# A hybrid decoder trunk on one core: high and low parts of v in one stationary tile, a PSUM bank per head, and the Fox heads' masks added by VectorE

## The chip, the cores and the metric

The kernel runs on one core of one Trainium2 chip. The metric is the device time of one execution in microseconds (us), lower is better. Three executions of the kernel before took 2653.26, 2653.28 and 2653.67 us; the median is 2653.28 us.

## What is computed

A trunk of two layers (512 tokens, 1024 channels, fp32) with three sub-layers in each: a SwiGLU feed-forward, a mixer, and a second feed-forward. The mixer projects the normed input once and feeds three branches: a gated linear recurrence, stick-breaking attention (8 heads of 64 channels) and forgetting attention ("Fox", 8 heads of 64). The change touches the two attentions, cut here to what matters:

```
# stick-breaking, per head, strictly causal (s < t)
z = q @ k.T * scale
w = exp(log_sigmoid(z) + suffix sums of log_sigmoid(-z)), 0 where s >= t
y = w @ v
# forgetting attention, per head
z = q @ k.T * scale + cum[t] - cum[s]
p = softmax(where(s <= t, z, -inf))
y = p @ v
# later: mixed += gate1 * (y_sb @ w_sb) + gate2 * (y_fox @ w_fox)
```

## The kernel before, in words

**Split numbers.** TensorE multiplies in the type fp32r, which keeps fewer bits than fp32. So every fp32 operand is held as a rounded high part and a low part (the rest), and a product is three matmuls into one PSUM bank: high by high, high by low, low by high (`mm3`, lines 1493 to 1496). Mostly ScalarE makes the high part, VectorE the low part, and each signals its own semaphore.

**Weights.** A unit is a weight tile of 128x8x128. SyncE loads it, ScalarE rounds it (`tick`, line 571), GpSimd subtracts (line 498), three units ahead of their use. A unit's 24 matmuls of 512 columns take TensorE about 5.4 us. ScalarE's program is written out by hand, so a tick stands at a fixed place among the attention's steps and runs when ScalarE gets there.

**Attention.** Each layer has 8 pairs of heads, p = 0 to 3 stick-breaking, p = 4 to 7 Fox. All engines run hand-ordered programs, each in its own order, and meet at semaphores. TensorE's order for a stick-breaking pair is:

```
scores(p); w_rg(2p); qkv(p+1, 0); qkv(p+1, 1); suffix(p, 0); suffix(p, 1)
turn_v(p); qkv(p+1, 2); w_rg(2p+1); values(p, 0); values(p, 1)
```

and for a Fox pair:

```
scores(p); gate1; qkv(p+1, 0); turn_v(p); turn(p, 0); turn(p, 1)
qkv(p+1, 1); values(p, 0); values(p, 1); qkv(p+1, 2)
```

`w_rg`, `qkv` and `gate1` are units, which fill the time in which ScalarE and VectorE work on the heads. `scores` (L1723) writes the scores of both heads to banks 4, 5, 6 (head 0) and 1, 2, 3 (head 1); for Fox pairs it then adds, per head, the decay (L1729, a picked row times ones) and the causal mask as identity times mask: three matmuls of 128, 256 and 128 columns. `suffix` (L1756, L1762) adds the stick-breaking sums, the last of them from `later_lo`, and `turn_v` (L1807) transposes v into bank 7; it waits for `k_lo` of the next pair. `turn` (L1775) transposes the Fox weights, normed by VectorE (`fx_norm`, L1343).

**Values.** `values(p, e)` is y of one head: four key blocks j with 512, 384, 256 and 128 query columns, `mm3` each, twelve matmuls. The stationary tile is 128 wide: the head's 64 columns of v, and zeros in the other 64, so both heads add into one bank (0 for stick-breaking, 7 for Fox) and each fills its own half of the partitions. Then `y_round` (ScalarE, L843) copies the bank to `ys_hi` or `yf_hi`, `y_rest` (VectorE, L1355) subtracts that from the bank, and the semaphore `ybl` says that y is done and the bank free.

**What follows y.** After `values(p-1, 1)` TensorE runs `scores(p)`, `w_rg(2p)` (bank 7) and `qkv(p+1, 0)` (bank 0, which waits for `ybl`). ScalarE goes on with a tick, then `sb_1` (absolute value L809, exp L811, ln L814 of head 0, then of head 1), a tick, `q_round`, a tick, `k_round`. VectorE goes on with `sb_softplus` (L1292 to L1306), `first_part` (L1363), `sb_sums` (L1313, L1315), the same of head 1, and in between `q_rest` (L1265) and `k_rest` (L1271, `k_lo`). For Fox pairs VectorE's `fx_max` (four row maxima per head, L1332) starts when all three banks of a head are done, ScalarE's `fx_1` (L828, exp) follows, then `fx_norm`.

Of the kernel before, what the change touches and what calls it, by code (L numbers as in the profile page):

```python
# [16 lines left out]
F32 = mybir.dt.float32  # L17
F32R = mybir.dt.float32r
# [136 lines left out]
def trunk(nc, w_units, ada_w, vecs, wf_in, wab, c_rows, x_in, out):  # L155
    with ExitStack() as ctx:
# [70 lines left out]
        ys_hi = at("ys_hi", 32768, [P, 4, T], F32R)  # L227
        ys_lo = at("ys_lo", 40960, [P, 4, T], F32R)
        part = at("part", 49152, [P, KD, T])

# [15 lines left out]
        k_lo = at("k_lo", 71680, [P, T], F32R)  # L246
        v_hi = at("v_hi", 73728, [P, TT, 2 * P], F32R)
        v_lo = at("v_lo", 77824, [P, TT, 2 * P], F32R)
        e_f = [at(f"e_f{i}", 81920 + 10240 * i, [P, NS]) for i in range(2)]
# [122 lines left out]
        vl = sig("vl", PAIRS)  # L372
        v_zero = sig("v_zero", 2)
        z_done = [sig(f"z_done{e}", 3 * PAIRS) for e in range(2)]
# [17 lines left out]
        pl = sig("pl", 3 * HEADS)  # L392
        pv_head = sig("pv_head", 2 * PAIRS)
        ybh = sig("ybh", PAIRS)
        ybl = sig("ybl", PAIRS)
# [162 lines left out]
        def _(act):  # L558
# [200 lines left out]
            def v_round(l, p):  # L759
                act.wait_ge(vt_done.sem, vt_done.at(l, p + 1))  # L760
                if p:
                    act.wait_ge(pv_head.sem, pv_head.at(l, 2 * p))
                if p == 0:
                    act.wait_ge(v_zero.sem, v_zero.at(l, 1))
                src = bank[7][:, :].rearrange("p (j e d) -> p j e d", j=TT, e=2)
                for e in range(2):
                    i = A(v_hi[:, :, e * (P + HD):e * (P + HD) + HD], src[:, :, e, :], ACT.Copy)
                i.then_inc(vh.sem, 1)
# [68 lines left out]
            def y_round(l, p):  # L837
                act.wait_ge(pv_head.sem, pv_head.at(l, 2 * p + 2))
                if p == 0:
                    act.wait_ge(yal.sem, yal.at(l, KD))  # L840
                if p == 4:
                    act.wait_ge(unit_done.sem, unit_done.at(l, U_WRG(KD - 1) + 1))
                A((ys_hi if p < 4 else yf_hi)[:, p % 4, :], bank[Y_BANK(p)][:, :], ACT.Copy).then_inc(ybh.sem, 1)  # L843

# [165 lines left out]
        def _(dve):  # L1010
# [263 lines left out]
            def v_rest(l, p):  # L1274
                if p == 0:
                    dve.wait_ge(v_zero.sem, v_zero.at(l, 2))
                dve.wait_ge(vh.sem, vh.at(l, p + 1))
                src = bank[7][:, :].rearrange("p (j e d) -> p j e d", j=TT, e=2)
                for e in range(2):
                    o = e * (P + HD)  # L1280
                    i = V.tensor_tensor(v_lo[:, :, o:o + HD], src[:, :, e, :], v_hi[:, :, o:o + HD].bitcast(F32),
                                        ALU.subtract)
                i.then_inc(vl.sem, 1)
# [42 lines left out]
            def fx_max(l, p, e):  # L1326
                n = 2 * (p - 4) + e
                dve.wait_ge(pv_head.sem, pv_head.at(l, 2 * p + e - 1))
                dve.wait_ge(z_done[e].sem, z_done[e].at(l, 3 * p + 3))
                for i in range(TT):  # L1330
                    b, o = FX_AT[i]
                    V.tensor_reduce(negmax[:, e, i:i + 1], bank[ZB[e][b]][:, o:o + P * (i + 1)], AX.X, ALU.max,  # L1332
                                    negate=True).then_inc(max_ready.sem, 1)
# [17 lines left out]

            def y_rest(l, p):
                dve.wait_ge(ybh.sem, ybh.at(l, p + 1))
                hi, lo = (ys_hi, ys_lo) if p < 4 else (yf_hi, yf_lo)
                V.tensor_tensor(lo[:, p % 4, :], bank[Y_BANK(p)][:, :], hi[:, p % 4, :].bitcast(F32),  # L1355
                                ALU.subtract).then_inc(ybl.sem, 1)
# [55 lines left out]
            for l in range(DEPTH):  # L1412
# [18 lines left out]
                V.memset(v_hi[:, :, :].bitcast(F32), 0.0).then_inc(v_zero.sem, 1)  # L1431
                V.memset(v_lo[:, :, :].bitcast(F32), 0.0).then_inc(v_zero.sem, 1)
                for p in range(4):
# [58 lines left out]
        def _(pe):  # L1492
# [199 lines left out]
            def scores(l, p):  # L1692
# [38 lines left out]
                for e in range(2):  # L1731
                    z = [bank[b] for b in ZB[e]]
                    if p >= 4:
                        h = pick[:, 2 * p + e - HEADS:2 * p + e - HEADS + 1].to_broadcast([P, P])
                        add(z[0], h, decay[:, :])
                        add(z[0][:, 3 * P:], ident_r[:, :], mask_fx[:, :]).then_inc(z_done[e].sem, 1)
                        add(z[1][:, 0:3 * P], h, decay[:, 0:3 * P])
                        add(z[1][:, 3 * P:], h, decay[:, 0:P])
                        add(z[1][:, 2 * P:], ident_r[:, :], mask_fx[:, :].unsqueeze(1).to_broadcast([P, 2, P])).then_inc(z_done[e].sem, 1)
                        add(z[2][:, 0:2 * P], h, decay[:, 0:2 * P])  # L1740
                        add(z[2][:, P:2 * P], ident_r[:, :], mask_fx[:, :]).then_inc(z_done[e].sem, 1)

# [100 lines left out]
            def w_rg(l, n):  # L1843
# [145 lines left out]

def Y_BANK(p):  # L1990
    return 0 if p < 4 else 7

# [116 lines left out]
```

## Time and profile before

| what | value |
|---|---|
| median of 3 executions | 2653.28 us |
| the profiled execution, its time | 2653.1 us |
| its span in the trace | 2651.3 us |
| TensorE busy | 2636.5 us, 99% |
| VectorE, ScalarE, GpSimd busy | 46%, 39%, 44% |
| mean granted TensorE clock | 0.999 |

The span is the time from the first to the last instruction of the trace; 1.8 us of the execution lie outside it. A matmul's busy time overlaps with the next one's, so the distance from one start to the next is what a matmul costs.

### The profile page before, as it was taken

Reading aid. Unit: us, or ns where it says so; the run is one execution under the profiler, and the core shown is the slowest. Engines: PE = TensorE matmul, PEld = TensorE weight load, DVE = VectorE, ACT = ScalarE, POOL = GpSimd, SP = SyncE. Lnnn points to the kernel's source line nnn. Section 1 sums busy time; section 2 is a strip of 40 time slices with the busy share of each in tenths; the row PEclk is TensorE's granted clock in tenths of the full one; section 3 lists DMA queues with packets and bytes.
Section 4 is the critical chain, followed back from the end, with each engine's and each line's share of the span. In section 5 each row is a group of like instructions: output and inputs, shape, how many; then the busy total and the mean of one; then the engine's idle time right before and its main releaser. Section 6 shows DMA issues by size and latency. Waiting matters only on the chain.

```text
span 2651.3 us, 31680 instructions
## 1 busy us (share of the span) xinstructions
PE 2636.5 (99%) x13012; PEld 2226.0 (84%) x13012; DVE 1232.2 (46%) x1666; ACT 1036.5 (39%) x1593; POOL 1167.6 (44%) x484
## 2 busy tenths in 40 slices
PE   9999999999999999999999999999999999999998
PEld 7888888888888898888898888988888888988887
DVE  6555337866642243411165553567755423453111
ACT  6222235675444243222242222466653432422222
POOL 5555544533223435544345554344332244454443
PEclk9999999999999999999999999999999999999999
DMA  8555532222122225423345555322221222253322
GB/s 315 197 196 191 169 133 81 99 75 72 64 64 80 90 80 190 143 96 103 96 168 190 196 201 168 102 81 96 80 68 61 64 96 95 84 199 126 101 96 80
DMA packets 90833, 323.81 MB, mean 122 GB/s; under 512 B 10048, under 2 KB 12480, under 8 KB 90432
## 3 DMA queue, kind: packets, MB, share of 16 engines
q1 hardware_dynamic: 90688, 321.78, 36.0%
q8 instruction: 103, 1.69, 0.3%
q14 instruction: 42, 0.34, 0.0%
HBM read 319.64 MB, written 2.10 MB: 121 GB/s over the span
## 4 chain that ended last, share of the span: by engine, by line
PE 98%; DMA 1%; DVE 1%; ACT 0%; SPq 0%; issue 0%; ACTq 0%; DVEq 0%
PE bank L1494 30%; PE bank L1496 30%; PE bank L1495 30%; PE bank L1529 3%; PE bank L1536 1%; PE bank L1723 1%; PE bank L1756 1%; PE bank L1775 1%; PE bank L1729 1%; DMA ada<-ada_w 1%; PE bank L1591 0%; PE bank L1807 0%; PE bank L1585 0%; PE bank L1579 0%; PE bank L1762 0%; PE bank L1571 0%
## 5 line engine op out<-in xcount | busy, mean ns | idle before, releaser
L498 POOL TENSOR_TENSOR w_lo<-raw,w_hi 128x1024 fp32r<-128x1024 f32 x434 | 1121.1, 2595 | 1340.2 <-ACT w_hi L571 1339.9
L1494 PE MATMUL bank<-h_hi,w_hi 128*128 128x512 f32 x2224 | 867.8, 390 | 0.1
L1496 PE MATMUL bank<-h_hi,w_lo 128*128 128x512 f32 x2224 | 865.6, 389 | 0.0
L1495 PE MATMUL bank<-h_lo,w_hi 128*128 128x512 f32 x2224 | 865.4, 389 | 0.0
L571 ACT ACTIVATE w_hi<-raw 128x1024 fp32r<-128x1024 f32 x434 | 458.5, 1058 | 928.5 <-PE bank L1496 830.2
L1496 PEld LDWEIGHTS bank<-h_hi,w_lo 128*128 128x128 f32 x2224 | 417.4, 188 | 86.9
L1494 PEld LDWEIGHTS bank<-h_hi,w_hi 128*128 128x128 f32 x2224 | 417.5, 188 | 86.3 <-issue 0.4
L1495 PEld LDWEIGHTS bank<-h_lo,w_hi 128*128 128x128 f32 x2224 | 417.6, 188 | 85.9
L1017 DVE CUSTOM_DVE_ANT_0 ada<-ada,c_act 128x1024 f32<-128x1024 f32 x144 | 241.9, 1688 | 256.3 <-DMA ada<-ada_w 256.3
L1494 PE MATMUL bank<-g_hi,w_hi 128*128 128x512 f32 (+1 forms) x792 | 290.1, 366 | 0.0
L1496 PE MATMUL bank<-g_hi,w_lo 128*128 128x512 f32 (+1 forms) x792 | 289.4, 365 | 0.0
L1495 PE MATMUL bank<-g_lo,w_hi 128*128 128x512 f32 (+1 forms) x792 | 289.4, 365 | 0.0
L1078 DVE SCALAR_TENSOR_TENSOR x<-bank,gatec,x 128x512 f32<-128x512 f32 (+1 forms) x56 | 37.4, 673 | 357.2 <-PE bank L1496 357.2
L1105 DVE TENSOR_TENSOR tmp<-tmp,bank 128x512 f32<-128x512 f32 x88 | 60.1, 684 | 241.0 <-ACT tmp L639 240.4
L1089 DVE TENSOR_TENSOR g_lo<-tmp,g_hi 128x512 fp32r<-128x512 f32 x88 | 170.7, 1943 | 0.0
L1494 PEld LDWEIGHTS bank<-g_hi,w_hi 128*128 128x128 f32 x792 | 149.3, 189 | 24.5
L1495 PEld LDWEIGHTS bank<-g_lo,w_hi 128*128 128x128 f32 x792 | 149.3, 189 | 24.1
L1496 PEld LDWEIGHTS bank<-g_hi,w_lo 128*128 128x128 f32 x792 | 149.3, 189 | 23.9
L1529 PE MATMUL bank<-h_hi,w_hi 128*128 128x256 f32 x320 | 86.9, 288 | 0.4
L1529 PE MATMUL bank<-h_hi,w_lo 128*128 128x256 f32 x320 | 85.1, 283 | 0.0
L1373 DVE TENSOR_TENSOR sg<-sg,bank 128x512 f32<-128x512 f32 x32 | 20.6, 684 | 137.4 <-PE bank L1496 137.4
L1536 PE MATMUL bank<-h_lo,w_hi 128*128 128x256 f32 x320 | 70.1, 283 | 0.0
(266 smaller groups left out, 3044.6 us busy)
## 6 DMA issues: line engine op xcount, KB each, us to landing
raw<-w_units SPq DMA_DIRECT2D x440, 512.0 KB, 3.4
ada<-ada_w SPq DMA_DIRECT2D x144, 512.0 KB, 4.5
ada<-ada_w SPq DMA_DIRECT2D x8, 1024.0 KB, 17.9
x<-x_in SPq DMA_DIRECT2D x4, 512.0 KB, 6.9
wab_raw<-wab SPq DMA_DIRECT2D x2, 1024.0 KB, 5.6
y<-fin SPq DMA_DIRECT2D x8, 256.0 KB, 2.3
c_act<-c_rows SPq DMA_DIRECT2D x1, 512.0 KB, 3.7
vec<-vecs SPq DMA_DIRECT2D x3, 92.5 KB, 3.1
```

The lines of the kernel that those rows point to most:

```text
L498: nc.gpsimd.tensor_tensor(w_lo[s][:, :, :], raw[u % RAW][:, :, :], w_hi[s][:, :, :].bitcast(F32), ALU.subtract).then_inc(unit_lo.sem, 1)
L571: A(w_hi[n % RING][:, :, :], raw[slot][:, :, :], ACT.Copy).then_inc(unit_hi.sem, 1)
L1017: V.tensor_tensor_reduce(ada[a % 2][:, :], ada[a % 2][:, :], c_act[:, :], 1.0, 0.0, ALU.mult, ALU.add, mod[:, col:col + 1]).then_inc(ada_d ...
L1078: V.scalar_tensor_tensor(out=x[:, n, cols], in0=bnk[:, at or cols], scalar=gatec[:, n:n + 1], in1=x[:, n, cols], op0=ALU.mult, op1=ALU.add ...
L1089: V.tensor_tensor(g_lo[:, f, :], tmp[2 + f % 2][:, :], g_hi[:, f, :].bitcast(F32), ALU.subtract).then_inc(gl_ready.sem, 1)
L1105: V.tensor_tensor(tmp[2 + f % 2][:, :], tmp[f % 2][:, :], bank[F_BANK(l, s, f) + 1][:, :], ALU.mult).then_inc(g_ready.sem, 1)
L1494: nc.tensor.matmul(o, wh, xh, start=start, stop=False, skip_group_check=True)
L1495: nc.tensor.matmul(o, wh, xl, start=False, stop=False, skip_group_check=True)
L1496: return nc.tensor.matmul(o, wl, xh, start=False, stop=stop, skip_group_check=True)
L1529: nc.tensor.matmul(bank[j][:, HALF[h]], w[(u + j) % RING][:, k, :], h_hi[:, k, HALF[h]], start=h == 0 and k == 0 and w is w_hi, stop=False ...
L1536: i = nc.tensor.matmul(bank[j][:, HALF[h]], w_hi[(u + j) % RING][:, k, :], h_lo[:, k, HALF[h]], start=False, stop=k == KD - 1, skip_group_ ...
L1723: m = nc.tensor.matmul(dst[e], left[lp][r, still], right[rp][r, moving], start=p >= 4 and o == 0 and lp == 0 and rp == 0, stop=False, skip ...
```

## The change

It has two parts. **v and y:** `v_hi` and `v_lo` become one tile `v_both`. A head's stationary tile holds the high part of v in its 64 columns and the low part in the other 64, where zeros were. `values` runs two matmuls per key block, with the high and the low part of the weights as moving operand, so the head's own half of the partitions gets v_hi times the weights and the other half gets v_lo times the weights. Each head has a bank of its own (0 and 7 for stick-breaking, 7 and 4 for Fox). ScalarE copies the low half of each head's bank to SBUF, VectorE adds the main half, ScalarE rounds the sum, VectorE subtracts. (v_lo times the low part of the weights, left out before, is in it now.) Three waits are new on TensorE: `w_rg(2p)` for `ybl` of the pair before, since it writes bank 7; `values(p, 1)` of stick-breaking pairs for `first_part` of unit w_rg(2p+1), which reads bank 7; and `scores(p)` from p = 5 on for `ybl`, since it writes bank 4. One of the two memsets of v is gone. **Masks:** the identity matmuls are gone, banks 0 and 2 get their decay before bank 1, and `fx_max` adds the mask in PSUM (three additions per head) before it takes the maxima, largest block first.

```diff
-        v_hi = at("v_hi", 73728, [P, TT, 2 * P], F32R)
-        v_lo = at("v_lo", 77824, [P, TT, 2 * P], F32R)
+        v_both = at("v_both", 73728, [P, TT, 2 * P], F32R)
...
             def y_round(l, p):
-                act.wait_ge(pv_head.sem, pv_head.at(l, 2 * p + 2))
...
-                A((ys_hi if p < 4 else yf_hi)[:, p % 4, :], bank[Y_BANK(p)][:, :], ACT.Copy).then_inc(ybh.sem, 1)
+                for e in range(2):
+                    act.wait_ge(pv_head.sem, pv_head.at(l, 2 * p + e + 1))
+                    main, low = slice(HD * e, HD * e + HD), slice(HD - HD * e, P - HD * e)
+                    A(y[main, p % 4, :], bank[Y_BANKS(p)[e]][low, :], ACT.Copy).then_inc(y_low.sem, 1)
+                act.wait_ge(y_sum.sem, y_sum.at(l, 2 * p + 2))
+                A(hi[:, p % 4, :], y[:, p % 4, :], ACT.Copy).then_inc(ybh.sem, 1)
...
             def v_rest(l, p):
...
-                    o = e * (P + HD)
-                    i = V.tensor_tensor(v_lo[:, :, o:o + HD], src[:, :, e, :], v_hi[:, :, o:o + HD].bitcast(F32),
-                                        ALU.subtract)
+                    o, low = e * (P + HD), HD * (1 + e)
+                    i = V.tensor_tensor(v_both[:, :, low:low + HD], src[:, :, e, :],
+                                        v_both[:, :, o:o + HD].bitcast(F32), ALU.subtract)
...
             def fx_max(l, p, e):
...
+                z = [bank[b] for b in ZB[e]]
+                diagonal = mask_fx[:, :].bitcast(F32)
+                two = z[1][:, 2 * P:].rearrange("p (i t) -> p i t", i=2)
+                dve.wait_ge(z_done[e].sem, z_done[e].at(l, 3 * p + 1))
+                V.tensor_tensor(z[0][:, 3 * P:], z[0][:, 3 * P:], diagonal, ALU.add).then_inc(z_masked.sem, 1)
+                dve.wait_ge(z_done[e].sem, z_done[e].at(l, 3 * p + 2))
+                V.tensor_tensor(z[2][:, P:2 * P], z[2][:, P:2 * P], diagonal, ALU.add).then_inc(z_masked.sem, 1)
                 dve.wait_ge(z_done[e].sem, z_done[e].at(l, 3 * p + 3))
-                for i in range(TT):
+                V.tensor_tensor(two, two, diagonal.unsqueeze(1).to_broadcast([P, 2, P]), ALU.add)\
+                    .then_inc(z_masked.sem, 1)
+                for i in (3, 1, 2, 0):
                     b, o = FX_AT[i]
+                    dve.wait_ge(z_masked.sem, z_masked.at(l, 3 * n + (3, 2, 3, 1)[i]))
...
             def y_rest(l, p):
+                for e in range(2):
+                    main = slice(HD * e, HD * e + HD)
+                    dve.wait_ge(y_low.sem, y_low.at(l, 2 * p + e + 1))
+                    V.tensor_tensor(y[main, p % 4, :], bank[Y_BANKS(p)[e]][main, :], y[main, p % 4, :],
+                                    ALU.add).then_inc(y_sum.sem, 1)
                 dve.wait_ge(ybh.sem, ybh.at(l, p + 1))
-                V.tensor_tensor(lo[:, p % 4, :], bank[Y_BANK(p)][:, :], hi[:, p % 4, :].bitcast(F32),
+                V.tensor_tensor(lo[:, p % 4, :], y[:, p % 4, :], hi[:, p % 4, :].bitcast(F32),
                                 ALU.subtract).then_inc(ybl.sem, 1)
...
             def scores(l, p):
+                    pe.wait_ge(ybl.sem, ybl.at(l, p))
...
-                        add(z[0], h, decay[:, :])
-                        add(z[0][:, 3 * P:], ident_r[:, :], mask_fx[:, :]).then_inc(z_done[e].sem, 1)
+                        add(z[0], h, decay[:, :]).then_inc(z_done[e].sem, 1)
+                        add(z[2][:, 0:2 * P], h, decay[:, 0:2 * P]).then_inc(z_done[e].sem, 1)
                         add(z[1][:, 0:3 * P], h, decay[:, 0:3 * P])
-                        add(z[1][:, 3 * P:], h, decay[:, 0:P])
...
+                        add(z[1][:, 3 * P:], h, decay[:, 0:P]).then_inc(z_done[e].sem, 1)
...
             def values(l, p, e):
+                    if e == 1:
+                        pe.wait_ge(part_ready.sem, part_ready.at(l, 2 * p + 2))
...
-                    i = mm3(bank[Y_BANK(p)][:, P * j:T], v_hi[:, j, e * P:e * P + P], v_lo[:, j, e * P:e * P + P],
-                            e_hi[e][:, src], e_lo[e][:, src], e == 0 and j == 0, False)
+                    for weights in (e_hi[e], e_lo[e]):
+                        i = nc.tensor.matmul(bank[Y_BANKS(p)[e]][:, P * j:T], v_both[:, j, e * P:e * P + P],
+                                             weights[:, src], start=j == 0 and weights is e_hi[e], stop=False,
+                                             skip_group_check=True)
...
             def w_rg(l, n):
                 elif n % 2 == 0:
                     pe.wait_ge(part_ready.sem, part_ready.at(l, n))
+                    pe.wait_ge(ybl.sem, ybl.at(l, n // 2))
...
-def Y_BANK(p):
-    return 0 if p < 4 else 7
+def Y_BANKS(p):
+    return (0, 7) if p < 4 else (7, 4)
```

## Rows read from the trace of the kernel before

**Rows 1.** The page, busy time of TensorE: engine, us (share), instructions.

```profile
PE   2636.5 (99%) x13012; PEld 2226.0 (84%) x13012; DVE 1232.2 (46%) x1666; ACT 1036.5 (39%) x1593; POOL 1167.6 (44%) x484
```

**Rows 2.** Timeline of TensorE, pair 0's values into pair 1's scores: start us, us.

```profile
582.99 0.39 PE L1494 MATMUL bank<-e_hi,v_hi 128*128 128x512 f32 x1
...
583.44 0.39 PE L1496 MATMUL bank<-e_hi,v_lo 128*128 128x512 f32 x1
583.67 0.33 PE L1494 MATMUL bank<-e_hi,v_hi 128*128 128x384 f32 x1
...
584.85 0.44 PE L1494 MATMUL bank<-e_hi,v_hi 128*128 128x512 f32 x1
...
586.65 0.27 PE L1496 MATMUL bank<-e_hi,v_lo 128*128 128x128 f32 x1
586.86 0.44 PE L1723 MATMUL bank<-q_hi,k_hi 64*128 64x384 f32 x2
...
588.96 0.50 PE L1494 MATMUL bank<-ya_hi,w_hi 128*128 128x512 f32 x1
```

**Rows 3.** Timeline of TensorE, first scores of pairs 2, 4 and 5.

```profile
625.30 0.44 PE L1723 MATMUL bank<-q_hi,k_hi 64*128 64x384 f32 x2
...
702.16 0.50 PE L1723 MATMUL bank<-k_hi,q_hi 64*128 64x512 f32 x2
...
734.74 0.49 PE L1723 MATMUL bank<-k_hi,q_hi 64*128 64x512 f32 x2
```

**Rows 4.** Timeline of TensorE, Fox pair 4, decay and mask of one head.

```profile
704.62 0.22 PE L1729 MATMUL bank<-mask_fx,ident_r 128*128 128x128 f32 x1
704.68 0.45 PE L1729 MATMUL bank<-decay,pick 128*128 128x384 f32 x2
704.96 0.34 PE L1729 MATMUL bank<-mask_fx,ident_r 128*128 128x256 f32 x1
705.13 0.28 PE L1729 MATMUL bank<-decay,pick 128*128 128x256 f32 x1
705.25 0.22 PE L1729 MATMUL bank<-mask_fx,ident_r 128*128 128x128 f32 x1
705.31 0.44 PE L1729 MATMUL bank<-decay,pick 128*128 128x512 f32 x1
```

**Rows 5.** Groups by form: count | busy us, mean ns | idle us before.

```profile
L1494 PE MATMUL bank<-e_hi,v_hi 128*128 128x512 f32 x32 | 13.3, 416 | 0.0
...
L1729 PEld LDWEIGHTS bank<-mask_fx,ident_r 128*128 128x128 f32 x48 | 9.0, 188 | 0.0
```

**Rows 6.** Timeline of ScalarE and of VectorE after pair 0's values.

```profile
586.96 0.60 ACT L843 ACTIVATE ys_hi<-bank 128x512 fp32r<-128x512 f32 x1 [3.97 <-PE bank L1496]
...
587.59 0.69 DVE L1355 TENSOR_TENSOR ys_lo<-bank,ys_hi 128x512 fp32r<-128x512 f32 x1 [3.72 <-ACT ys_hi L843]
```

**Rows 7.** Groups by form: a copy and two subtractions.

```profile
L1379 DVE TENSOR_TENSOR mx_lo<-part,mx_hi 128x512 fp32r<-128x512 f32 x16 | 11.1, 693 | 11.2 <-ACT mx_hi L869 11.2
...
L869 ACT ACTIVATE mx_hi<-part 128x512 fp32r<-128x512 f32 x16 | 10.1, 632 | 93.6 <-DVE part L1377 93.6
...
L1349 DVE TENSOR_TENSOR e_lo<-bank,e_hi 128x256 fp32r<-128x256 f32 x16 | 6.6, 413 | 0.0
```

**Rows 8.** Timelines of GpSimd, VectorE and TensorE in pair 1.

```profile
601.80 2.50 POOL L498 TENSOR_TENSOR w_lo<-raw,w_hi 128x1024 fp32r<-128x1024 f32 x1 [1.55 <-ACT w_hi L571]
...
601.63 0.42 DVE L1298 TENSOR_TENSOR later<-e_f 128x256 f32<-128x256 f32 x1
601.97 2.42 DVE L1300 COPY later<-e_f 128x128 f32<-128x128 f32 x1
...
609.22 0.68 DVE L1271 TENSOR_TENSOR k_lo<-bank,k_hi 128x512 fp32r<-128x512 f32 x1
...
610.05 0.63 PE L1807 MATMUL bank<-ident,vt 128*128 128x128 f32 x4
```

**Rows 9.** Timelines of VectorE and TensorE in Fox pair 4, weights normed and turned.

```profile
711.73 3.46 DVE L1343 TENSOR_SCALAR e_f<-e_f,rsums 128x128 f32<-128x128 f32 x4
...
717.71 2.35 PE L1775 MATMUL bank<-ident,e_f 128*128 128x128 f32 x20
```

More of the change, by code:

```diff
@@ L228, in trunk @@
         ys_lo = at("ys_lo", 40960, [P, 4, T], F32R)
+        ys_f = at("ys_f", 40960, [P, 4, T])
+        yf_f = at("yf_f", 8192, [P, 4, T])
         part = at("part", 49152, [P, KD, T])
@@ L372, in trunk @@
         vl = sig("vl", PAIRS)
-        v_zero = sig("v_zero", 2)
+        v_zero = sig("v_zero", 1)
         z_done = [sig(f"z_done{e}", 3 * PAIRS) for e in range(2)]
@@ L393, in trunk @@
         pv_head = sig("pv_head", 2 * PAIRS)
+        y_low = sig("y_low", 2 * PAIRS)
+        y_sum = sig("y_sum", 2 * PAIRS)
+        z_masked = sig("z_masked", 3 * HEADS)
         ybh = sig("ybh", PAIRS)
@@ L766, in v_round @@
                 for e in range(2):
-                    i = A(v_hi[:, :, e * (P + HD):e * (P + HD) + HD], src[:, :, e, :], ACT.Copy)
+                    i = A(v_both[:, :, e * (P + HD):e * (P + HD) + HD], src[:, :, e, :], ACT.Copy)
                 i.then_inc(vh.sem, 1)
@@ L837, in y_round @@
             def y_round(l, p):
-                act.wait_ge(pv_head.sem, pv_head.at(l, 2 * p + 2))
+                hi, y = (ys_hi, ys_f) if p < 4 else (yf_hi, yf_f)
                 if p == 0:
@@ L1275, in v_rest @@
                 if p == 0:
-                    dve.wait_ge(v_zero.sem, v_zero.at(l, 2))
+                    dve.wait_ge(v_zero.sem, v_zero.at(l, 1))
                 dve.wait_ge(vh.sem, vh.at(l, p + 1))
@@ L1352, in y_rest @@
             def y_rest(l, p):
+                hi, lo, y = (ys_hi, ys_lo, ys_f) if p < 4 else (yf_hi, yf_lo, yf_f)
+                for e in range(2):
[3 more added lines that the diff above has]
+                                    ALU.add).then_inc(y_sum.sem, 1)
                 dve.wait_ge(ybh.sem, ybh.at(l, p + 1))
-                hi, lo = (ys_hi, ys_lo) if p < 4 else (yf_hi, yf_lo)
-                V.tensor_tensor(lo[:, p % 4, :], bank[Y_BANK(p)][:, :], hi[:, p % 4, :].bitcast(F32),
+                V.tensor_tensor(lo[:, p % 4, :], y[:, p % 4, :], hi[:, p % 4, :].bitcast(F32),
                                 ALU.subtract).then_inc(ybl.sem, 1)
@@ L1430, in _ @@
                         forget_2(l)
-                V.memset(v_hi[:, :, :].bitcast(F32), 0.0).then_inc(v_zero.sem, 1)
-                V.memset(v_lo[:, :, :].bitcast(F32), 0.0).then_inc(v_zero.sem, 1)
+                V.memset(v_both[:, :, :].bitcast(F32), 0.0).then_inc(v_zero.sem, 1)
                 for p in range(4):
@@ L1734, in scores @@
                         h = pick[:, 2 * p + e - HEADS:2 * p + e - HEADS + 1].to_broadcast([P, P])
-                        add(z[0], h, decay[:, :])
-                        add(z[0][:, 3 * P:], ident_r[:, :], mask_fx[:, :]).then_inc(z_done[e].sem, 1)
+                        add(z[0], h, decay[:, :]).then_inc(z_done[e].sem, 1)
+                        add(z[2][:, 0:2 * P], h, decay[:, 0:2 * P]).then_inc(z_done[e].sem, 1)
                         add(z[1][:, 0:3 * P], h, decay[:, 0:3 * P])
-                        add(z[1][:, 3 * P:], h, decay[:, 0:P])
-                        add(z[1][:, 2 * P:], ident_r[:, :], mask_fx[:, :].unsqueeze(1).to_broadcast([P, 2, P])).then_inc(z_done[e].sem, 1)
-                        add(z[2][:, 0:2 * P], h, decay[:, 0:2 * P])
-                        add(z[2][:, P:2 * P], ident_r[:, :], mask_fx[:, :]).then_inc(z_done[e].sem, 1)
+                        add(z[1][:, 3 * P:], h, decay[:, 0:P]).then_inc(z_done[e].sem, 1)
             def suffix(l, p, e):
```

## The prediction

> **What bounds the kernel now.** I read the page first, then the timelines of TensorE, VectorE, ScalarE and GpSimd through the attention, then the groups by form for durations. TensorE is busy for 2636.5 of 2651.3 us [rows 1], and that is real work there: in the values of pair 0 each matmul starts when its predecessor's columns have passed, 0.45 us for the two of 512 columns from 582.99 and 0.23 us for the third [rows 2]. The row groups give the same picture: between pair 1's and pair 2's scores lie 38.44 us (586.86 to 625.30), between pair 4's and pair 5's 32.58 us [rows 2, 3], and in neither did I find TensorE idle for longer than the 0.10 us at a change from 128 to 64 rows (586.65 plus the last matmul's 0.11 us, to 586.86). So a matmul taken out is time gained, as long as no other engine's chain comes out later than TensorE's order wants it. That second half is where the risk lies, because TensorE meets chains of ScalarE and VectorE with little to spare.
>
> **Values: removed work.** Before, a pair's 24 matmuls run from 582.99 to 586.86, less the 0.10 us of the change of rows: 3.77 us. One of three goes. By time a third of 3.77 us is 1.26 us per pair, 0.63 us per head. From below, only the columns count: 1280 columns at 0.23 us per 512 are 0.57 us. I take 0.63 us, since short matmuls cost more than their columns here (a head takes 1.86 us, 582.99 to 584.85, where 3 x 1280 columns would take 1.70 us). The group of the 512-column block has 32 members [rows 5], one per head, so 32 x 0.63 = **20.2 us** (18.2 at the low end). The two matmuls of a block share their stationary tile, but so did the first two of `mm3`, and they were no cheaper than the third.
>
> **Masks: removed work.** The identity matmuls occupy 0.06, 0.17 and 0.06 us by distance of starts (704.62 to 704.68, 704.96 to 705.13, 705.25 to 705.31) [rows 4]. That is 0.29 us; the matmul behind a short one starts later than its own columns explain by some 0.05 us, so I take 0.34 us. There are 48 such weight loads [rows 5], three per head, 16 heads: **5.4 us**. Low end by columns, 512 at 0.23 us: 3.7 us.
>
> The work removed is 25.6 us (low end 21.9). Dropping one memset, placing v_lo in another tile and swapping banks cost nothing on TensorE: the memset is VectorE's, before pair 0, and v_lo's two subtractions keep their shapes.
>
> **The y chain: added work.** Before: last matmul start 586.65, ScalarE's copy 586.96 to 587.56, VectorE's subtraction 587.59 to 588.28 [rows 6], hidden behind scores, w_rg only started at 588.96 [rows 2] and did not need it. Now w_rg(2p) waits for it, and the chain has four links behind the last matmul. (Head 0's low copy and addition run during head 1's matmuls, 1.25 us long.) ScalarE copies head 1's low half from 586.96, with 64 partitions but 512 columns, so I price it like the full copy; VectorE adds from 587.59 for 0.69 us; ScalarE rounds from 588.31 for 0.63 us, VectorE subtracts from 588.97 for 0.69 us [rows 7] (both SBUF to SBUF); TensorE goes at 589.75 instead of 588.96. **Stall one: 0.79 us**. It strikes pairs 1, 2 and 3 of each layer, six times: pair 0 has no y before it, pair 4 has `gate1` where w_rg stood, 1.3 us of decay later. Queued behind the wait is all of TensorE.
>
> The other queue that pays is ScalarE's: its rounding starts at 588.31 instead of 586.96, so the tick, then abs, exp and ln of both heads come 1.35 us later, and VectorE's softplus work with them. Its end is `k_lo`, done at 609.90, and `turn_v` starts at 610.05 [rows 8]. Nearly nothing is spare. TensorE itself is 0.79 us late, so the chain may slip by 0.8 to 0.9 us for free. By the rows it slips by more, though not 1.35 us: VectorE's copy L1300 sat from 601.97 to 604.39, where GpSimd's subtraction ran from 601.80 to 604.30 [rows 8]. That GpSimd piece follows `q_round`, hence TensorE, and moves to 602.59 to 605.09; L1298 moves from 601.63 to 602.98, now falls behind GpSimd's start, and waits with L1300. Both end at about 605.65 in place of 604.39: a slip of 1.26 us, `k_lo` at 611.16 against a TensorE that wants it at 610.84, plus some 0.08 us to wake. **Stall two: 0.4 us**, in the same six pairs. Together 1.2 us, **7.2 us** in all. Ends: 0.79 x 6 = 4.7 us if the softplus chain makes it; 1.35 us plus 0.1 us for a reload after the stop, 8.7 us, if it slips in full.
>
> For Fox pairs the chain of y takes the same 2.8 us, hidden by `qkv(p+1, 2)`, 5.4 us; without that cover it would be another 0.8 us or more each. At the end of pair 7 a gate unit gives the same cover. The new wait in `values(p, 1)` is met: `first_part` needs 0.9 us from the end of w_rg, `values(p, 0)` takes 1.23 us. If not, it costs the difference.
>
> **Mask additions: added work.** VectorE gets three per head. The nearest row is a 128x256 operation out of PSUM, 0.41 us [rows 7]; 128 columns I estimate at 0.28 us, so below 1.0 us per head, and the first two run beside TensorE's decay matmuls. I expect head 1's maxima 1.0 us later. Spare: VectorE's normed weights of head 1 are done at 715.19 and the turns, 2.35 us for both heads, begin at 717.71 [rows 9], so head 1's begin at 718.89, 3.7 us later; 0.7 us of that goes with the removed masks. Cost nothing, from 0 to 5.4 us.
>
> **The sum.** 20.2 + 5.4 - 7.2 = 18.4 us. The profiled execution took 2653.1 us (span 2651.3), 0.2 us under the median, which I neglect: 2653.1 - 18.4 = **2634.7 us**. Own range of this case, from 21.9 - 8.7 and 25.6 - 4.7: 2632 to 2640.
>
> **A rule against it.** VectorE's last link read PSUM and SBUF before and now reads two SBUF tiles. Rows: of VectorE's work the SBUF copy L1300 took 2.42 us beside GpSimd [rows 8]. The Trainium skill, SBUF — State Buffer, "Who interferes with whom", says the same of any VectorE instruction with two SBUF inputs against GpSimd work that reads SBUF, and that one with a single SBUF input is spared. By it `y_rest` becomes exposed. GpSimd works only after a tick, and ScalarE's next tick stands behind `y_round`, so I expect GpSimd idle then.
>
> **Rivals.**
> - *All stalls hidden* (0.08): ScalarE or VectorE is quicker on 64 partitions. 2653.1 - 25.6 = 2627.5. Against it: the four links in the rows add up.
> - *GpSimd in the way of y* (0.07): the last subtraction waits once for a GpSimd piece of 2.50 us in each of the six pairs. 15 us more: 2649.7. Against it: the order of the tick.
> - *Masks late* (0.12): VectorE's fx_max plus a GpSimd piece (L1343 took 3.46 us for four short operations [rows 9]) eats the 3.0 us to spare and the mask gain with it: 2634.7 + 5.4 = 2640.1.
> - *Slower* (0.03): TensorE in `turn_v` or w_rg waits for VectorE behind two GpSimd pieces in a row, 5.0 us per pair, six pairs, 30 us: 2664.7. It decides from 18.4 / 6 = 3.1 us more per pair. The rows show single pieces there.
> - *The split does not do as it says* (0.02): the second matmul on a tile skips its load and short ones get 0.05 us cheaper, 32 heads: 1.6 us, 2633.1.
>
> **How the numbers follow.** The forecast has 0.68. The range 2630 to 2641 takes it in with its bounds, the late masks and part of the hidden stalls, and leaves out some 0.17. A measurement of this kernel can tell about 0.2%, 5.3 us, from no change: below 2648.0 is faster. Faster: 0.68 + 0.08 + 0.12 + 0.02 = 0.90; same: 0.07; slower: 0.03.
>
> **What would show it.** Values per pair about 2.5 us; scores to scores about 30.6 us for Fox pairs (32.58 - 1.26 - 0.68) and about 38.4 us for pairs 1 to 3, where gain and stalls nearly cancel; w_rg's first matmul 2.9 us after scores began, not 2.1; a gap before `turn_v`; VectorE's L1298, not L1300, held by GpSimd. I am wrong if the stick-breaking pairs shrink by over 1 us or grow, or if gaps stand before `turn` or in Fox scores.

## The result and the profile after

Four executions of the changed kernel took 2632.69 us in the median (2632.56 to 2634.20); four of the kernel before on the same chip took 2653.27 us (2652.98 to 2653.67). The ratio is 0.9922, 95% interval 0.9909 to 0.9934: **20.6 us less**. The profiled execution took 2632.58 us, its span is 2630.6 us. One execution of the kernel before, out of seven in a later session, took 3685.04 us at a mean granted clock of 0.668, and the ratios of that session are taken without it.

The page of the kernel after; against [rows 1] TensorE has 176 matmuls fewer (128 of the values, 48 of the masks), and is still busy for 99% of the span:

```profile
span 2630.6 us, 31452 instructions
PE 2611.4 (99%) x12836; PEld 2201.3 (84%) x12836; DVE 1260.7 (48%) x1744; ACT 1056.8 (40%) x1625; POOL 1167.3 (44%) x484
```

The timeline of TensorE, kernel after: start in us, busy us, then the instruction and in brackets what ended the idle time before it. It answers to [rows 2] and to the last row of [rows 8].

```profile
582.69 0.39 PE L1818 MATMUL bank<-e_hi,v_both 128*128 128x512 f32 x1
582.92 0.39 PE L1818 MATMUL bank<-e_lo,v_both 128*128 128x512 f32 x1
583.14 0.33 PE L1818 MATMUL bank<-e_hi,v_both 128*128 128x384 f32 x1
...
585.06 0.27 PE L1818 MATMUL bank<-e_lo,v_both 128*128 128x128 f32 x1
585.26 0.44 PE L1747 MATMUL bank<-q_hi,k_hi 64*128 64x384 f32 x2
...
588.18 0.47 PE L1517 MATMUL bank<-ya_hi,w_hi 128*128 128x512 f32 x1 [0.74 <-issue]
...
609.05 0.34 PE L1783 MATMUL bank<-later_lo,nones_r 128*128 128x384 f32 x1
609.46 0.63 PE L1832 MATMUL bank<-ident,vt 128*128 128x128 f32 x4
```

Two matmuls stand on each block of the values instead of three, so the pair's values run from 582.69 to 585.26 with the 0.10 us of the change of rows: 2.47 us of work instead of 3.77. Then comes the new wait: w_rg starts 2.92 us after the pair's scores (588.18 to 585.26) instead of 2.10, and TensorE stood for 0.74 us. That unit reads `ya`, the result of the recurrence, and not the y of attention: it waits only because it writes bank 7, which y's last readers must have left. The last two rows show the second, small gap: the 384 columns of 609.05 have passed by about 609.22, `turn_v` starts at 609.46.

The chain of y on ScalarE and on VectorE, kernel after (for [rows 6]); two timelines, one fence each:

```profile
585.37 0.59 ACT L850 ACTIVATE ys_f<-bank 64x512 f32<-64x512 f32 x1 [0.61 <-PE bank L1818]
586.73 0.63 ACT L852 ACTIVATE ys_hi<-ys_f 128x512 fp32r<-128x512 f32 x1 [0.76 <-DVE ys_f L1376]
```

```profile
586.00 0.70 DVE L1376 TENSOR_TENSOR ys_f<-bank,ys_f 64x512 f32<-64x512 f32 x1 [0.52 <-ACT ys_f L850]
587.39 0.69 DVE L1379 TENSOR_TENSOR ys_lo<-ys_f,ys_hi 128x512 fp32r<-128x512 f32 x1 [0.70 <-ACT ys_hi L852]
```

Four links, each waiting for the one before: copy 585.37, addition 586.00, rounding 586.73, subtraction 587.39 to 588.08, w_rg at 588.18. The two on 64 partitions cost as much as those on 128 (0.59 us against 0.60 for the copy out of PSUM [rows 6], 0.70 against 0.69 on VectorE).

The middle of pair 1 on GpSimd and on VectorE, kernel after (for [rows 8]); L1307, L1309 and L1280 of after are L1298, L1300 and L1271 of before:

```profile
600.99 2.39 POOL L502 TENSOR_TENSOR w_lo<-raw,w_hi 128x1024 fp32r<-128x1024 f32 x1 [0.94 <-ACT w_hi L575]
```

```profile
601.43 2.23 DVE L1307 TENSOR_TENSOR later<-e_f 128x256 f32<-128x256 f32 x1
603.59 0.21 DVE L1309 COPY later<-e_f 128x128 f32<-128x128 f32 x1
...
608.63 0.68 DVE L1280 TENSOR_TENSOR k_lo<-bank,k_hi 128x512 fp32r<-128x512 f32 x1
```

Now L1307 starts behind GpSimd's piece and is held for 2.23 us (0.42 before), and the copy follows it, 0.21 us, where it was held itself before.

VectorE in Fox pair 4, kernel after: the three mask additions of head 0, the four row maxima, and the normed weights of head 1 (for [rows 9]).

```profile
702.54 0.30 DVE L1342 TENSOR_TENSOR bank<-bank,mask_fx 128x128 f32<-128x128 f32 x1
702.75 0.29 DVE L1344 TENSOR_TENSOR bank<-bank,mask_fx 128x128 f32<-128x128 f32 x1
702.95 0.42 DVE L1346 TENSOR_TENSOR bank<-bank,mask_fx 128x256 f32<-128x256 f32 x1
703.28 1.67 DVE L1351 TENSOR_REDUCE negmax<-bank 128x1 f32<-128x512 f32 x4
...
709.70 3.47 DVE L1362 TENSOR_SCALAR e_f<-e_f,rsums 128x128 f32<-128x128 f32 x4
```

The additions cost 0.74 us (702.54 to 703.28); head 1's weights are done at 713.17, and TensorE's turns start at 714.56, head 1's at about 715.74.

**Where the 20.6 us came from**, by the starts of each pair's scores (548.12, 585.26, 623.42, 661.56, 699.70 and 730.32 us in layer 1; layer 2 repeats them):

| From scores to scores | before | after | difference | times |
|---|---|---|---|---|
| pair 0 | 38.45 | 37.14 | -1.31 | 2 |
| pairs 1, 2, 3 | 38.44 | 38.15 | -0.29 | 6 |
| Fox pairs 4 to 7 | 32.58 | 30.61 | -1.97 | 8 |

In pair 0 `w_rg(0)` has no y of a pair before it to wait for, so this pair shows the values alone: 1.31 us per pair, 21.0 us in 16 pairs. The Fox pairs show the masks on top: 1.97 - 1.31 = 0.66 us, 5.3 us in 8 pairs. Pairs 1 to 3 show the stalls: 1.31 - 0.29 = 1.02 us, 6.1 us in six pairs. (Pair 7 has no scores behind it; its 1.97 us is taken over from pairs 4 to 6.) 21.0 + 5.3 - 6.1 = 20.2 us; another 0.3 us lies before the first pair's scores (548.12 against 548.41), ahead of all changed work, where the runs of this study scatter from 547.3 to 549.5.

### The profile page after: what moved, and what is told of

It reads as the page before. It is cut to its first block, busy times and chain, and to the rows that moved or that the text cites. A ratio compares the mean times of both kernels' runs of the same rounds, so it can differ in the third digit from the quotient of the medians.

```text
span 2630.6 us, 31452 instructions
## 1 busy us (share of the span) xinstructions
PE 2611.4 (99%) x12836; PEld 2201.3 (84%) x12836; DVE 1260.7 (48%) x1744; ACT 1056.8 (40%) x1625; POOL 1167.3 (44%) x484
## 4 chain that ended last, share of the span: by engine, by line
PE 98%; DVE 1%; DMA 1%; issue 0%; ACT 0%; SPq 0%; ACTq 0%; DVEq 0%
PE bank L1517 29%; PE bank L1518 29%; PE bank L1519 29%; PE bank L1552 3%; PE bank L1818 2%; PE bank L1559 1%; PE bank L1747 1%; PE bank L1777 1%; PE bank L1796 1%; DMA ada<-ada_w 1%; PE bank L1753 0%; PE bank L1832 0%; PE bank L1614 0%; PE bank L1602 0%; PE bank L1608 0%
## 5 line engine op out<-in xcount | busy, mean ns | idle before, releaser
L1397 DVE TENSOR_TENSOR sg<-sg,bank 128x512 f32<-128x512 f32 x32 | 20.6, 685 | 133.6 <-PE bank L1519 133.6
```

## The experiments

Unless an interval is given, a time is that of one execution, with a profile beside it. The kernels ran in three sessions, each beside the kernel before: 2653.33 us (one execution) beside the first four kernels below; 2654.55 us in the median of seven beside both edits, the tick behind three pairs, the added wait and the fourfold additions; 2653.28 us beside the other three. "Per pair" is the distance from scores to scores; it repeats within 0.04 us from pair to pair and layer to layer where nothing else is said, while the first scores of a kernel come anywhere from 547.3 to 549.5 us. So small differences are read from the pairs.

### Values alone, masks alone

The first kernel is the one after, with the masks of before:

```
-  V.tensor_tensor(z[0][:, 3 * P:], z[0][:, 3 * P:], diagonal, ALU.add)
...
+  add(z[0][:, 3 * P:], ident_r[:, :], mask_fx[:, :]).then_inc(z_done[e].sem, 1)
...
```

> The changed kernel with its masks put back on TensorE as identity matmuls. Theory (work on TensorE less the waits behind y): the values lose 1.31 us in each of 16 pairs, 21.0 us, and six pairs pay 1.0 us, so 2653.1 - 14.9 = about 2638.0 us; Fox pairs 31.3 us apart. Rival (the mask additions cost or bring something else than their matmuls): the difference to the changed kernel's 2632.7 us is not 5.3 us.

Measured: 2638.88 us; Fox pairs 31.30 us, pairs 1 to 3 38.15, pair 0 37.15. The total is 6.2 us over the kernel after, where 5.3 were expected; of the 0.9 us too much 0.4 lie before the first scores (548.50 against 548.12), 0.2 are in the Fox pairs, and the rest is not traced. The second is the kernel before with only the additions on VectorE in place of those matmuls (v, y and banks as before):

> The kernel before with only the masks moved to VectorE. Theory: 16 heads x 0.33 us, 5.3 us, nothing given back: 2647.8 us; Fox pairs 31.9 us apart, stick-breaking pairs unchanged at 38.44 us. Rival (VectorE's additions come late somewhere): less than 5 us, and a gap before the turns.

Measured: 2647.87 us; Fox pairs 31.88 instead of 32.58, pairs 0 to 3 at 38.44 as before. So the masks are worth 0.69 us per pair with either layout of the values (31.30 - 30.61, 32.58 - 31.88), 5.5 us, and the two halves of the change don't touch each other: every stall comes with the values.

### The first stall: what w_rg waits for

It reads nothing of y: it overwrites bank 7, and the last instruction that reads y there is VectorE's addition of head 1. The rounding and the subtraction behind it work in SBUF, so the wait for `ybl` is two links longer than the bank needs. Here TensorE waits for the addition instead:

```
-                    pe.wait_ge(ybl.sem, ybl.at(l, n // 2))
+                    pe.wait_ge(y_sum.sem, y_sum.at(l, n))
```

> The changed kernel, but w_rg(2p) waits for VectorE's addition, the last reader of bank 7, instead of for ybl two steps later. Theory of two stalls in one place each: the 0.8 us before w_rg go, ScalarE stays as late as it was, so VectorE's k_lo comes late against a TensorE that is now on time; GpSimd's second piece goes back with TensorE by 0.8 us, so the slip is about 0.3 to 0.4 us and turn_v stalls 0.25 to 0.4 us: 0.6 to 0.8 us per pair gained, 3.6 to 4.8 us, about 2628.5 us. Rival (the slip of ScalarE's chain sets the end and the stall only moves to turn_v): under 1 us gained, gap before turn_v about 1 us.

Measured: 2628.03 us, pairs 1 to 3 at 37.49 us. w_rg starts 2.11 us after the scores, as before the change. Stall one is thus worth 38.15 - 37.49 = 0.66 us per pair. The rest, 37.49 - 37.14 = 0.35 us, stays, with the gap of 0.24 us before `turn_v` at its old size and some 0.1 us in front of the last `suffix` matmuls. What TensorE meets there is `k_lo`: in the kernel before, the one after and this one `turn_v` starts 0.15 us behind the end of `k_lo`, and `k_lo` starts 22.36, 23.37 and 22.71 us behind the scores. The 0.35 us are the difference of the first and the last. VectorE's row in this kernel says where it arises:

```profile
600.80 1.58 DVE L1307 TENSOR_TENSOR later<-e_f 128x256 f32<-128x256 f32 x1
```

With scores at 584.63, it ends 17.75 us behind them, and before the change the held copy ended 17.53 us behind them (604.39 less 586.86): 0.22 us. The copy, which before was itself the held instruction, now comes behind it, another 0.13 us: 0.35 us.

### The rounding on VectorE: a shorter chain that costs 16.5 us

ScalarE makes the two low copies only; VectorE rounds y behind its own addition, so one hand-over less. ScalarE is free 1.28 us earlier (its tick starts 0.72 us behind the scores in pair 1 instead of 2.00).

```
-                act.wait_ge(y_sum.sem, y_sum.at(l, 2 * p + 2))
-                A(hi[:, p % 4, :], y[:, p % 4, :], ACT.Copy).then_inc(ybh.sem, 1)
...
+                dve.wait_ge(y_sum.sem, y_sum.at(l, 2 * p + 2))
+                V.tensor_copy(hi[:, p % 4, :], y[:, p % 4, :]).then_inc(ybh.sem, 1)
```

> The changed kernel, but VectorE rounds y (between its addition and its subtraction), and ScalarE goes on after its two low copies. Theory: ScalarE's tick and softplus chain come 1.35 us earlier, the gap before turn_v goes (0.24 us x 6); the chain to w_rg gets shorter by 0.2 us (0.43 us of VectorE in place of 0.63 us of ScalarE): about 2.6 us gained, 2630.1 us. Rival (what sets the end is ScalarE's slip, w_rg's wait is hidden behind it): over 5 us gained.

Measured: 2649.22 us; pairs 1 to 3 at 39.85 to 41.46 us. The expected time was missed by 19 us, and the result is 16.5 us worse than the kernel after. The timelines of ScalarE, GpSimd, VectorE and TensorE of this kernel, pair 1:

```profile
585.25 1.06 ACT L575 ACTIVATE w_hi<-raw 128x1024 fp32r<-128x1024 f32 x1
...
586.39 2.35 POOL L502 TENSOR_TENSOR w_lo<-raw,w_hi 128x1024 fp32r<-128x1024 f32 x1 [2.29 <-ACT w_hi L575]
...
585.99 0.43 DVE L1377 CAST ys_hi<-ys_f 128x512 fp32r<-128x512 f32 x1
586.46 2.84 DVE L1379 TENSOR_TENSOR ys_lo<-ys_f,ys_hi 128x512 fp32r<-128x512 f32 x1
...
589.39 0.47 PE L1517 MATMUL bank<-ya_hi,w_hi 128*128 128x512 f32 x1 [2.69 <-issue]
```

This is the rival "GpSimd in the way of y", which the kernel after escapes. ScalarE, done early, runs its tick at 585.25 and so hands GpSimd a piece at 586.39; VectorE's subtraction of two SBUF tiles starts 0.07 us behind it and takes 2.84 us instead of 0.69. In the kernel after the tick stands behind the rounding, and GpSimd's piece starts at 588.38, 0.30 us after the subtraction has ended:

```profile
588.38 2.41 POOL L502 TENSOR_TENSOR w_lo<-raw,w_hi 128x1024 fp32r<-128x1024 f32 x1 [3.59 <-ACT w_hi L575]
```

And a second price follows. Windows on TensorE of this kernel: stretch, its length, busy us and matmuls, granted clock, share and GB/s of the DMA.

```profile
575.00:585.00 10.00, 10.00 (x54) 1.00 0.40 135
...
589.00:592.50 3.50, 3.11 (x8) 0.63 0.46 150
...
595.00:605.00 10.00, 10.00 (x46) 1.00 0.17 52
...
1898.10:1901.60 3.50, 3.10 (x14) 1.00 0.44 150
```

```profile
590.39 0.63 PE L1517 MATMUL bank<-ya_hi,w_hi 128*128 128x512 f32 x1
590.81 0.63 PE L1518 MATMUL bank<-ya_lo,w_hi 128*128 128x512 f32 x1
...
1898.50 0.47 PE L1517 MATMUL bank<-ya_hi,w_hi 128*128 128x512 f32 x1 [2.69 <-issue]
```

After the stop of 2.69 us TensorE ran at the lower of its two clock levels: matmuls of 512 columns start 0.42 us apart (590.39 to 590.81) where they start 0.23 us apart at the full one (582.69 to 582.92 in the kernel after), for some 3.3 us. In the kernel after the granted clock behind its stop of 0.74 us is 1.00. But the low clock doesn't follow every such stop: all six are 2.69 us long, and behind the one that ends at 1898.50 (layer 2, pair 1) the granted clock is 1.00, with 14 matmuls in the 3.50 us where the first stop is followed by 8. That pair takes 39.85 us, its stop and nothing more; the five others take 41.16 to 41.46. So a stop costs its 2.69 us, and in five cases of six 1.3 to 1.6 us more. What sets the sixth apart no run here shows.

To tell the tick's place from the rounding on VectorE as the cause, the next kernel keeps the edit and gives ScalarE one wait more, ahead of its tick:

```
+                act.wait_ge(ybh.sem, ybh.at(l, p + 1))
```

> As e4_cast_dve, but ScalarE waits for VectorE's rounding of y before its next tick, so GpSimd's piece can't start before VectorE's subtraction. In e4 the subtraction took 2.84 us, GpSimd had started 0.07 us before it, and TensorE ran at half clock after the 2.7 us stop. Theory (GpSimd's start in front of the subtraction is the whole of e4's loss): the subtraction takes 0.69 us again, w_rg starts 2.7 us after scores (2.9 in the changed kernel), no half-clock rows, ScalarE still 1.1 us late: 2630 to 2632 us. Rival (rounding on VectorE is itself slow, or the half clock has another cause): stays above 2640 us.

Measured: 2630.53 us, pairs 1 to 3 at 37.95 us, w_rg 2.71 us behind the scores; no low clock. One wait took back 18.7 us, as forecast.

### Both edits together

> VectorE rounds y as in e4, and w_rg(2p) waits for the addition only, as in e3. Theory: GpSimd still holds VectorE's subtraction up by 2.2 us, but nothing waits for it until qkv(p+1, 0), 5 us later, and ScalarE's softplus chain starts 1.35 us earlier than in e3, so the gap before turn_v goes: 0.35 us x 6 under e3_wait_sum, about 2626.0 us, pairs 1 to 3 at 37.15 us like pair 0. Rival (the held subtraction delays VectorE's softplus, which comes 0.5 us behind it): gap before turn_v stays, 2628 us or more.

Measured, four executions each: 2627.39 us (2626.48 to 2627.85), ratio to the kernel before 0.9901 (0.9883 to 0.9918); pairs 1 to 3 at 37.30 us. VectorE's timeline, pair 2 of this kernel:

```profile
623.78 2.89 DVE L1379 TENSOR_TENSOR ys_lo<-ys_f,ys_hi 128x512 fp32r<-128x512 f32 x1
```

The subtraction is held as in the kernel with the rounding on VectorE alone, but no one waits for it: w_rg waits for the sum. What lengthens an instruction costs nothing until something waits for its end. The result lies between the forecast and its rival: a gap of 0.13 us before `turn_v` is left, pairs 1 to 3 miss 37.15 us by 0.15 us, and the time is 1.4 us over the 2626.0 expected.

### The tick moved ahead of y

If GpSimd's piece is in the way, let it run earlier. w_rg's tick of the next pair goes ahead of the rounding of y, on top of both edits; first behind pairs 0, 1 and 2:

```
-                    if p:
-                        tick(l, U_WRG(2 * p))
...
+                    if p < 3:
+                        tick(l, U_WRG(2 * p + 2))
```

> As e5_both, and ScalarE's tick for unit w_rg(2p+2) stands before y_round, so it runs during the values of head 0 or before, and GpSimd's piece is over when y comes. Theory: the subtraction is no longer held (0.7 us), but since nothing waited for it, no time is gained over e5: 2626.0 us within 0.5. Rival (e5 still loses time by the held subtraction): 1 us or more under e5.

Measured: 2628.56 us (2628.17 to 2629.06), ratio 0.9904 (0.9889 to 0.9920): slower by 1.2 us than the kernel with both edits beside it, where no difference was expected. Pairs 2 and 3 do come down to 37.15 us, but pair 1 takes 38.57 and 38.34. ScalarE's timeline, then TensorE's, pair 1 of this kernel:

```profile
585.51 1.06 ACT L575 ACTIVATE w_hi<-raw 128x1024 fp32r<-128x1024 f32 x1 [3.41 <-DMA raw<-w_units]
586.59 1.21 ACT L850 ACTIVATE ys_f<-bank 64x512 f32<-64x512 f32 x2
```

```profile
588.73 0.47 PE L1517 MATMUL bank<-ya_hi,w_hi 128*128 128x512 f32 x1 [1.41 <-issue]
```

The tick behind pair 0 waited for its weights' transfer, with y's copies behind it. So it was left where it was for pair 1, and moved for pairs 2 and 3 only:

```
-                    if p:
+                    if p == 1:
...
+                    if p in (1, 2):
+                        tick(l, U_WRG(2 * p + 2))
```

> As e5_both, with the earlier tick of e8_all only after pairs 1 and 2; in e8 the one after pair 0 stood 3.4 us in a wait for its weights' transfer, ScalarE's low copies of y behind it, and w_rg 1.4 us behind those, while pairs 2 and 3 ran at 37.15 us. Theory: pair 1 at 37.30 us as in e5, pairs 2 and 3 at 37.15 us: 0.6 us under e5_both, 2626 to 2627 us, a ratio of 0.990 to the kernel before. Rival (the early tick costs elsewhere, too): not under e5.

Measured: **2626.50 us** (2625.94 to 2627.97), ratio to the kernel before 0.9901 (0.9885 to 0.9918). Pairs 2 and 3 are at 37.15 us, the distance of pair 0, which has no stall: nothing is left there of what the change had added. Pair 1 keeps 0.14 us. The kernel is 26.8 us under the kernel before, where the change alone is 20.6 us under it; from the kernel with both edits its time can't be told, only its profile.

Last, the same tick with the rounding left on ScalarE: does the early tick alone close the gap before `turn_v`?

> ScalarE rounds y as in the changed kernel, w_rg(2p) waits for the addition only as in e3, and the tick stands before y_round after pairs 1 and 2. Theory (what makes turn_v late is ScalarE's slip of 1.35 us, of which the tick takes 1.05 us away): pair 1 at 37.49 us as in e3, pairs 2 and 3 at 37.15 us, no gap before turn_v there: 1.4 us under e3, 2626.5 to 2627.5 us. Rival (the gap before turn_v is GpSimd's doing whatever ScalarE does): 37.49 us in all three.

Measured: 2629.16 us (2628.22 to 2630.03), ratio 0.9910 (0.9895 to 0.9924); pair 1 at 37.49 us, pairs 2 and 3 at 37.40 us, and the gap of 0.24 us stands in all of them. The rival held in the main: of the 0.34 us the tick was to bring, it brought 0.09. (That the total lies 1.1 us over that of the kernel with the new wait alone is not the tick's doing: the first scores come 2.0 us later here, 549.51 to 547.48.) GpSimd and VectorE of this kernel, pair 2, and VectorE and GpSimd of the kernel above at the same place:

```profile
639.13 2.39 POOL L502 TENSOR_TENSOR w_lo<-raw,w_hi 128x1024 fp32r<-128x1024 f32 x1 [1.15 <-ACT w_hi L575]
...
639.36 2.44 DVE L1309 TENSOR_TENSOR later<-e_f 128x256 f32<-128x256 f32 x1
```

```profile
636.60 0.42 DVE L1307 TENSOR_TENSOR later<-e_f 128x256 f32<-128x256 f32 x1
...
636.89 2.39 POOL L502 TENSOR_TENSOR w_lo<-raw,w_hi 128x1024 fp32r<-128x1024 f32 x1 [1.68 <-ACT w_hi L575]
```

The gap of 0.24 us is there when VectorE's 256-column instruction comes behind GpSimd's start (by 0.44 us in the kernel after, 1.18 with the new wait, 0.60 with the added wait, 0.23 here), and not there when it comes ahead by 0.17 us (before the change [rows 8]) or 0.29 us (pairs 2 and 3 of the best kernel). In between stand the kernel with both edits, ahead by only 0.05 us, with a gap of 0.13, and pair 1 of the best, ahead by 0.09, with 0.09; there GpSimd's piece took 2.62 and 2.59 us instead of 2.39. The kernel with the rounding on VectorE alone doesn't count: TensorE was 4 us late there, and `k_lo` was ready 3.1 us before it. Moving this one instruction by itself wasn't tried, so its part in the gap rests on this comparison.

### How much room the masks have

Twice and four times the additions of every head. The mask is added that many times over. One thing more differs from the kernel after: the first addition waits until all three banks of the head are done, and each row maximum waits for all additions. The diff of the twofold kernel (the other has 4, 12 and 12 for 2, 6 and 6):

```
+                for r in range(2):
+                    if r:
+                        dve.wait_ge(z_masked.sem, z_masked.at(l, 6 * n + 3 * r))
...
+                    dve.wait_ge(z_masked.sem, z_masked.at(l, 6 * n + 6))
```

> The changed kernel with the mask additions made twice. In e6 three extra rounds made head 1's weights 5.7 us later, 1.9 us per round, and g1_copy as much, on which turn_v waits with 3.1 us to spare. Theory (2.5 us to spare at the turns, 3.1 us at turn_v): one extra round costs nothing, 2632.7 us within 1, Fox pairs at 30.6 us. Rival (each round costs, 36 us / 3 rounds): 2640 us or more.

Measured: 2633.07 us, Fox pairs 30.59 to 30.70 us: a second round costs nothing. It makes head 1's weights 2.3 us later: 12.27 us behind pair 4's scores (711.19 less 698.92) instead of 10.00.

> The changed kernel with the three mask additions of a Fox head made four times in a row (the masked scores become more negative, the weights stay the same), some 0.75 us more per round and head, 4.5 us later for head 1. Theory (2.5 us to spare in the changed kernel between VectorE's normed weights and head 1's turn, so one round costs nothing): it exceeds the spare time by about 2 us in each of 8 Fox pairs, with a gap between or before the turns: 14 to 20 us more, 2647 to 2653 us. Rival (the spare time is larger, the masks are far from mattering): within 2 us of 2632.7. Rival 2 (none to spare): over 30 us more.

Measured: 2668.69 us, 36 us over the kernel after; Fox pairs 33.91 to 35.04 us, the others unchanged at 38.15. The time forecast, 2647 to 2653 us, was missed by 16 us. By the number alone the second rival (no room at all) would have it, but a second round costs nothing, and that rules it out. VectorE reached head 1's weights 5.7 us later (715.42 against 709.70): 2.3 us for the first extra round with its later start, 1.7 for each of the others. But the turns were not the first to run dry. ScalarE, then TensorE of this kernel, pair 4:

```profile
716.00 0.70 ACT L858 ACTIVATE sg<-bank,vec 128x512 f32<-128x512 f32 x1
```

```profile
716.84 0.63 PE L1835 MATMUL bank<-ident,vt 128*128 128x128 f32 x4 [2.55 <-ACT sg L858]
717.30 3.98 PE L1799 MATMUL bank<-ident,e_f 128*128 128x128 f32 x20
```

and the windows of its TensorE around it:

```profile
703.00:713.00 10.00, 10.00 (x47) 1.00 0.00 0
...
716.00:721.00 5.00, 4.16 (x25) 0.68 0.29 90
...
786.00:791.00 5.00, 3.77 (x28) 1.00 0.27 88
```

`turn_v` waits for a copy of ScalarE that stands behind both heads' weights in ScalarE's queue. In the kernel after that copy is done at 710.98, 3.1 us ahead of `turn_v`; here it came 2.55 us late, and behind that stop the clock was low again: the turns took 3.98 us instead of 2.35. Three rounds more are 5.7 us, less 3.1 us of room is 2.6 us, and the stop is 2.55 us. That is so in six of the eight Fox pairs; in pair 7 of each layer another copy of ScalarE (L868) holds `turn_v`, for 3.97 us. Behind pair 6's stop, the last row shown, the clock stayed at 1.00 in both layers, and these pairs take 33.91 us where pairs 4 and 5 take 34.78 to 35.04. The 36 us are 4.5 us per Fox pair in the mean: the stop, and behind six stops of eight the low clock.

## Why the prediction was right, and where it was off

It gave 2634.7 us (2630 to 2641), 18.4 us of gain; it was 2632.7 us and 20.6 us. The mechanism held: which work goes, which two waits come, and that nothing else does. The sizes that were off, the second stall above all, were off to the same side.

- **Values**, forecast 0.63 us per head, 20.2 us: 0.655 us and 21.0 us. Short matmuls gave back slightly more than a third of the time.
- **Masks**, forecast 0.34 us per head, 5.4 us: 0.345 us and 5.5 us, by the two kernels with one part each.
- **Stall one**, forecast 0.79 us, w_rg at 2.9 us behind the scores: 2.92 us. The step was right: the lateness stays in full down to the last `suffix` matmul, which starts 23.79 us behind the scores instead of 23.01, 0.78 us later. Its removal brings only 0.66 us, because the second stall then grows from 0.23 to 0.35 us. What the prediction didn't see is that it was needless: w_rg reads no y, and the bank is free two links earlier.
- **Stall two**, forecast 0.4 us: 0.24 us, and this is the mis-sized term. The step was "Both end at about 605.65 in place of 604.39: a slip of 1.26 us". L1307 was held, as said, but the slip is 1.01 us: `k_lo` starts 23.37 us behind the scores instead of 22.36. GpSimd's piece took 2.39 us and not 2.50, and VectorE's last held work ended 0.42 us behind it (603.80 to 603.38), not 0.56. One size worked the other way: from the end of `k_lo` to `turn_v` it takes 0.15 us, not 0.08. Both stalls together: 6.1 us, not 7.2.
- **Mask additions**, cost 0: right, and the twofold kernel shows that weights another 2.3 us later cost nothing either. Their price was right too, 0.74 us for a head with the 128-column ones at 0.29 us, but not the room. The step "3.7 us later" looked at the turns; head 1's turn has 2.5 us left with the additions in (713.17 to 715.74), and in the fourfold kernel `turn_v`, with 3.1 us, was the first to stop.
- **The rule against it** was rightly weighed: GpSimd was idle then, because the tick stands behind the rounding in ScalarE's queue. The rounding on VectorE takes that cover away, and the rival came true. That it cost 16.5 us, where the rival had 15, is luck in part: the rival counted one wait of 2.50 us per pair, and what was measured is a stop 1.95 us longer plus, in five of six pairs, the low clock. The prediction gives the Trainium skill's section (SBUF — State Buffer, "Who interferes with whom") too widely: an instruction with one SBUF input is spared there only outside the modes that use both ports. The SBUF copy L1300, with one input, was held for 2.42 us [rows 8]. *All stalls hidden* would have been 2627.5 us; the kernels that remove both stalls, but for 0.14 us in some pairs, reach 2626.5 and 2627.4.

## What to carry to other kernels

Where one engine is never idle, work taken out of it is gained by the instruction, and what has to be counted is the chain that now ends later: add up its links and look for the first place at which the full engine wants its end, also through a third engine's queue. Where an instruction waits only to overwrite a buffer, let it wait for the buffer's last reader, not for the end of the chain that this reader belongs to (0.66 us per pair here, for one line). An engine relieved early issues its next work early: before moving work off it, look at what that work sets off, and against whom it then runs.

## What was not expected of the hardware

- **Who starts first decides who pays.** A VectorE instruction on two SBUF tiles that came 0.07 us behind GpSimd's start took 2.84 us instead of 0.69; one of 0.42 us that came 0.29 us ahead of it lost nothing, but the copy right behind that one, 0.05 us behind GpSimd's start, took 2.42 us instead of 0.21. Additions out of PSUM ran through beside GpSimd undisturbed, in the kernel with the early tick and the rounding on ScalarE (GpSimd, then VectorE, behind pair 1):

```profile
622.97 2.39 POOL L502 TENSOR_TENSOR w_lo<-raw,w_hi 128x1024 fp32r<-128x1024 f32 x1 [2.08 <-ACT w_hi L575]
```

```profile
623.61 0.68 DVE L1378 TENSOR_TENSOR ys_f<-bank,ys_f 64x512 f32<-64x512 f32 x1 [1.15 <-ACT ys_f L850]
...
624.87 0.69 DVE L1378 TENSOR_TENSOR ys_f<-bank,ys_f 64x512 f32<-64x512 f32 x1 [0.58 <-ACT ys_f L850]
```

  The Trainium skill, SBUF — State Buffer, "Who interferes with whom", has VectorE and GpSimd share one pair of ports under an exclusive lock, which an instruction with at most one SBUF input does not need outside the modes that use both ports. These rows agree: 0.68 and 0.69 us beside a piece that ran from 622.97 to 625.36, and 2.84 us with two.
- **A stop can cost more than itself, but need not.** Behind five of six stops of 2.69 us and behind four of six of 2.55 us TensorE ran at its lower clock level (granted clock 0.63 and 0.68 over the first stretches shown), as it did behind both of 3.97 us; behind the other three, with the same instructions in front, it was 1.00. Behind the stops of 0.74 and 1.41 us it was 1.00 too. The low clock added 1.3 to 1.6 us to a pair in the kernel with the rounding on VectorE. Why it fails to come behind some stops stays open.
- **Half the partitions cost the same.** 64 x 512 took 0.59 us on ScalarE and 0.70 on VectorE, 128 x 512 took 0.60 (L843 before the change, out of PSUM as well) and 0.69.
